# One step of a hybrid decoder on one core: the squares of a sublayer's input go to TensorE one block at a time, without VectorE's sum of two

## The chip, the core and the metric

The kernel runs on one core of one Trainium2 chip. Five engines work from programs of their own and meet only at semaphores: TensorE (PE in the profile, PEld for its weight loads), VectorE (DVE), ScalarE (ACT), GpSimd (POOL) and SyncE (SP), which issues most of the transfers. The metric is the device time of one execution in microseconds (us).

## What is computed

One inference step of a trunk with two layers. Layer 0 is gated linear attention and a convolutional FFN, layer 1 is multi-head latent attention and a convolutional FFN. There are 544 tokens: a prompt of 512 and 8 sequences of 4 new tokens each. The model width is 1024. Around every sublayer stand two norms, one on its input and one on its output:

```python
def rmsnorm(x, g):
    xf = x.astype(jnp.float32)
    y = xf * lax.rsqrt(jnp.mean(xf * xf, axis=-1, keepdims=True) + EPS)
    return (y * g.astype(jnp.float32)).astype(x.dtype)
...
        x = x + rmsnorm(mix, p['norm_mix_post'][l])
        h = rmsnorm(x, p['norm_ffn_pre'][l])
        f, buf = conv_ffn(h, conv_s0[l], p['ffn_w_gate'][l], p['ffn_w_up'][l], p['ffn_conv_w'][l],
                          p['ffn_conv_b'][l], p['ffn_w_down'][l])
        conv_bufs.append(buf)
        x = x + rmsnorm(f, p['norm_ffn_post'][l])
```

What matters here is the mean of x*x over the 1024 channels, one number per token, for the norm on a sublayer's input.

## The kernel before

**Layout.** Channels lie on the 128 partitions, in DC = 8 blocks, and tokens along the free dimension, 544 of them in two halves of HALF = 272. So a sum over channels is a sum over partitions and blocks. TensorE makes it by multiplying with a 128x128 matrix of ones (`ones_matmuls`, line 2128: one matmul for each half, which the program runs as two passes, so that a step shows as x4 in the profile) and adding up the blocks in PSUM, in `px`. ScalarE turns it into rstd = (mean + eps)^-0.5 by a logarithm and an exponential (`rstd`, lines 817 to 822).

**Precision.** Weights and inputs of the large products are split into a high and a low part. A tile of 128 output channels takes, for each of the 8 blocks of input, three products (high by high, high by low, low by high) in two halves: six matmuls (`tile_matmuls`, line 2063) into the bank set `lin`. The input parts are `xg_h` (ACT, line 802, x times the gain) and `xg_l` (DVE, line 1341). rstd is not in them; it is multiplied in where the products leave PSUM, so products can start before rstd is known, but can't leave without it. The weight panels are split too: ACT makes `w_h` (line 791), POOL makes `w_l` (line 669), in two slots each.

**The stage of the change** is the passage from one sublayer to the next. It is gone through with this code in three places: before the first ConvFFN (norm number n = 2, near 302 us), before the latent attention (n = 4, near 703 us) and before the second ConvFFN (n = 8, near 1119 us). Each engine has its own order, written by hand in its part of the program:
- DVE (`next_input`): for block after block, the next-but-one block's normed output `tb` (line 1517), `xg_l` of this block, and x + tb (line 1523). After every second block it adds the squares of the two blocks (line 1572).
- ACT (`next_input`): for each block `xg_h`, then its square into `sq` (line 808). `sq` has two buffers, used in turn. ACT waits on the semaphore `sq_used` until the buffer of the square two before is free.
- PE (`first_panels`): the tile matmuls of the first weight panel as the blocks' `xg_l` arrive; after every second block the ones matmuls on the sum of two squares (`pair_squares`). The tile matmuls of the second panel run LAG = 4 blocks behind. Only the first two blocks' first halves were made ahead, at the end of the stage before.

The norms that are summed in this way are in BY_PAIR; the others go another way, by a running sum in `ssq` and the function `stat`. SQ_BASE and SQ_LEN count the squares through the whole program, and `sq_used` goes up by one for each square: for a pair, once by DVE's sum and once by the ones matmuls.

```python
                    act.wait_ge(sq_used, i - 1)
                fn(sq[:, i % 2, :], src, ACT.Square).then_inc(sq_done, 1)
```

Behind the stage, in a ConvFFN, eight plain panels run on PE, while DVE, ACT and POOL make operands for the paired products that follow (line 2349). The third panel waits until DVE has taken the first tile out of PSUM, with rstd (lines 1595 to 1597). Before the latent attention, ACT makes rstd and then copies the third weight panel.

Of the kernel before, what the change touches and what calls it, by code (L numbers as in the profile page):

```python
# [20 lines left out]
ALU = mybir.AluOpType  # L21
# [5 lines left out]
DC = D // P  # L27
# [66 lines left out]
SQ_BASE = [0, 8, 16, 24, 32, 40, 42, 45, 53, 61]  # L94
SQ_LEN = [8, 8, 8, 8, 8, 2, 3, 8, 8, 8]
# [28 lines left out]
def trunk_program(nc, io):  # L124
    ctx = ExitStack()
    with ctx:
        def sem(name):
            return ctx.enter_context(nc.semaphore(name))
# [12 lines left out]
        def keep(name, shape, dt=F32):  # L141
            off = pos[0]
            pos[0] += (4 * int(np.prod(shape[1:])) + 31) // 32 * 32
            return at(name, off, shape, dt)
# [16 lines left out]
        sq = keep("sq", [P, 2, NT])  # L161
# [126 lines left out]
        def col(name, k=0, n=1):  # L288
            return par[:, PCOL[name] + k:PCOL[name] + k + n]
# [11 lines left out]
        sq_done, sq_used = sem("sq_done"), sem("sq_used")  # L301
# [163 lines left out]

        BY_PAIR = (2, 4, 8)
        DVE_LAST = (0, 3, DC - 1)
        LAG = 4  # L470

        def sums_before(n):

            return sum(k not in BY_PAIR for k in range(n))

        sc_bank = (banks[1], banks[7], banks[0], banks[2])

# [9 lines left out]
        def rest(ch, ahead=AHEAD):  # L487

            return second if ch < ahead else slice(0, NT)
# [816 lines left out]
        def _(dve):  # L1306
            v = nc.vector
# [212 lines left out]
            def add_residual(event, ch):  # L1520
                dve.wait_ge(t_done, DC * event + ch + 1)
                tok = rest(ch)
                v.tensor_tensor(x[:, ch, tok], x[:, ch, tok], tb[:, ch % 2, tok], ALU.add).then_inc(x_done, 1)  # L1523
# [32 lines left out]
            def next_input(event, n, t_last, y, y_gain, split_event, gain, i0):  # L1556
                dve.wait_ge(rstd_done, n + 1)
                residual(event, n, t_last, y, y_gain, 0)
                residual(event, n, t_last, y, y_gain, 1)
                add_residual(event, 0)  # L1560
                add_residual(event, 1)
                for ch in range(DC):
                    if ch < DC - 2:
                        residual(event, n, t_last, y, y_gain, ch + 2)
                    split_x_lo(xg_h, xg_l, ch, col(gain[0], gain[1] + ch), DC * split_event + ch + 1,
                               rest(ch))
                    if ch < DC - 2:
                        add_residual(event, ch + 2)
                    if ch % 2:
                        i = i0 + ch  # L1570
                        dve.wait_ge(sq_done, i + 1)
                        v.tensor_tensor(sq[:, i % 2, :], sq[:, (i - 1) % 2, :], sq[:, i % 2, :], ALU.add).then_inc(sq_used, 1)

            def ffn(layer, pa, ta, pb, tb_, n_stat):
                f0, us0, ps_, ts_ = layer * FC, layer * US_ALL, pa + 2 * PLAIN, ta + 2 * PLAIN
# [471 lines left out]
        def _(pe):  # L2047
# [47 lines left out]
            def first_panels(p, t, arrive, n, halves_from=None):  # L2095

                take_panel(p)
                free_set(t)  # L2100
                if halves_from is not None:
                    for k in range(AHEAD):
                        pe.wait_ge(h_lo, AHEAD * (halved(halves_from) - 1) + k + 1)
                        tile_matmuls(p % 2, t % 2, xg_h, xg_l, (k,), w0=k, start=k == 0, stop=False, halves_=(0,))
                for k in range(DC + LAG):
                    if k < DC:
                        part = dict(w0=k, start=k == 0, stop=k == DC - 1)
                        if halves_from is not None and k < AHEAD:
                            part["halves_"] = (1,)
                        pe.wait_ge(xl_done, arrive + k + 1)  # L2110
                        last = tile_matmuls(p % 2, t % 2, xg_h, xg_l, (k,), **part)
                        if k == DC - 1:
                            last.then_inc(w_used, 1)
                        if n in BY_PAIR and k % 2:
                            pair_squares(n, k)
                    if k == DC and n not in BY_PAIR:
                        stat(n)
                    if k == LAG:
                        take_panel(p + 1)
                        free_set(t + 1)  # L2120
                    if k >= LAG:
                        j = k - LAG
                        last = tile_matmuls((p + 1) % 2, (t + 1) % 2, xg_h, xg_l, (j,), w0=j, start=j == 0, stop=j == DC - 1)
                last.then_inc(w_used, 1)

            def ones_matmuls(src, start, stop):
                for half in range(2):
                    last = mm(px[:, half, 0:HALF], ones[:], src[:, half * HALF:(half + 1) * HALF], start=start, stop=stop)  # L2128
                return last

            def pair_squares(n, k):

                if k == 1:
                    pe.wait_ge(stat_ln, n)
                pe.wait_ge(sq_used, SQ_BASE[n] + k)
                ones_matmuls(sq[:, (SQ_BASE[n] + k) % 2, :], k == 1, k == SQ_LEN[n] - 1).then_inc(sq_used, 1)

            def stat(n):

# [705 lines left out]
```

## Time and profile before

| | us |
|---|---|
| median of 3 runs | 1530.73 |
| lowest and highest | 1529.43, 1531.11 |
| the profiled execution | 1527.54 |
| its span | 1525.8 |
| PE busy (share of the span) | 1446.5 (95%) |
| PE weight loads busy | 1320.1 (87%) |
| DVE busy | 921.5 (60%) |
| ACT busy | 675.2 (44%) |
| POOL busy | 564.2 (37%) |

The span is the time between the first and the last recorded work; the execution's own time is 1.7 us more. Each number in a profile comes from this one execution. A busy share is a mean over stages with different limits, so what counts for an edit is which wait ends last in its own stage. Matmul ends are modelled, and overlap: the distance from one start to the next tells what one costs in a row, and the duration of one also holds its drain. PEclk is the granted clock of TensorE as a share of 2.4 GHz. "[1.62 <-DVE sq L1572]" behind a row means that the engine was idle for 1.62 us before it, until DVE's instruction of line 1572 on `sq` released it.

### The profile page before, as it was taken

To read this page: it belongs to the slowest core of one execution; us is meant where nothing else is said; L and a number is where in the kernel's file an instruction comes from. 1 tells how busy PE (TensorE), PEld (TensorE's weight loads), DVE (VectorE), ACT (ScalarE), POOL (GpSimd) and SP (SyncE) were. 2 spreads that over 40 slices of the span, in tenths; PEclk is the share of its full clock that TensorE was granted. 3 is DMA by queue.
4 is the path that set the end of the run, shared out by engine and by line. 5 is a ranking of instruction groups with operands and counts; after the bars stand their busy time and mean duration, and the time that the engine had idled before them with its cause. 6 is when DMAs were issued, how large, how long until landed. Compare 5 with 4: busy or idle time off the path is not lost.

```text
span 1525.8 us, 31329 instructions
## 1 busy us (share of the span) xinstructions
PE 1446.5 (95%) x11260; PEld 1320.1 (87%) x11260; DVE 921.5 (60%) x1496; ACT 675.2 (44%) x1263; POOL 564.2 (37%) x561
## 2 busy tenths in 40 slices
PE   6999999899999999998899999998979999999997
PEld 6999998799999999997886556665969999999996
DVE  4632436589888882225657744443579888885223
ACT  5333435355666662215412544443254566665211
POOL 2432113335445444341330044441425454544333
PEclk9999999999999999999999999999999999999999
DMA  4242222213232322223221089980212323222221
GB/s 160 71 138 97 111 70 97 88 56 108 87 110 82 110 76 77 95 84 113 75 91 45 1 264 285 284 260 29 84 47 97 111 82 110 82 76 94 95 89 70
DMA packets 55610, 160.20 MB, mean 105 GB/s; under 512 B 7553, under 2 KB 25474, under 8 KB 54226
## 3 DMA queue, kind: packets, MB, share of 16 engines
q1 hardware_dynamic: 49362, 137.82, 27.3%
q0 software_dynamic: 6144, 20.98, 4.6%
q8 instruction: 67, 1.10, 0.3%
q14 instruction: 37, 0.30, 0.1%
HBM read 150.72 MB, written 8.05 MB: 104 GB/s over the span
## 4 chain that ended last, share of the span: by engine, by line
PE 78%; DVE 12%; ACT 4%; issue 3%; POOL 1%; DMA 0%; SPq 0%; ACTq 0%; DVEq 0%; POOLq 0%
PE lin L2063 36%; PE lin L2349 22%; PE lin L2545 4%; PE px L2622 2%; PE px L2586 2%; PE px L2533 1%; PE px L2590 1%; DVE x L1523 1%; DVE tb L1517 1%; PE px L2262 1%; PE px L2553 1%; PE px L2128 1%; DVE xg_l L1341 1%; PE lin L2499 1%; DVE c L1586 1%
## 5 line engine op out<-in xcount | busy, mean ns | idle before, releaser
L674 POOL TENSOR_TENSOR w_l<-w_raw,w_h 128x1024 fp32r<-128x1024 f32 (+1 forms) x62 | 174.6, 2815 | 355.7 <-ACT w_h L791 234.2
L2063 PE MATMUL lin<-xg_h,w_h 128*128 128x272 f32 x960 | 224.1, 309 | 34.1 <-DVE xg_l L1341 26.0
L2063 PE MATMUL lin<-xg_l,w_h 128*128 128x272 f32 x960 | 208.5, 292 | 0.0
L2063 PE MATMUL lin<-xg_h,w_l 128*128 128x272 f32 x960 | 208.1, 292 | 0.0
L2063 PEld LDWEIGHTS lin<-xg_h,w_h 128*128 128x128 f32 x960 | 158.1, 193 | 46.9 <-DVE xg_l L1341 20.2
L2349 PE MATMUL lin<-xq_h,wq_r 128*128 128x272 f32 x864 | 179.9, 296 | 5.5 <-ACT part L1040 5.4
L669 POOL TENSOR_TENSOR w_l<-w_raw,w_h 128x1024 fp32r<-128x1024 f32 (+2 forms) x39 | 98.0, 2513 | 214.0 <-ACT w_h L791 214.0
L791 ACT ACTIVATE w_h<-w_raw 128x1024 fp32r<-128x1024 f32 (+2 forms) x77 | 83.6, 1087 | 210.2 <-PE lin L2063 191.6
L2349 PE MATMUL lin<-xq_h,w_h 128*128 128x272 f32 x576 | 166.2, 289 | 0.3
L2349 PE MATMUL lin<-xq_h,w_l 128*128 128x272 f32 x576 | 166.0, 288 | 0.0
L2349 PE MATMUL lin<-xq_l,w_h 128*128 128x272 f32 x576 | 165.4, 287 | 0.0
L2063 PEld LDWEIGHTS lin<-xg_l,w_h 128*128 128x128 f32 x960 | 157.7, 193 | 0.3
L2063 PEld LDWEIGHTS lin<-xg_h,w_l 128*128 128x128 f32 x960 | 156.4, 192 | 0.0
L2063 PE MATMUL lin<-a_h,w_h 128*128 128x272 f32 x704 | 152.1, 293 | 4.5 <-DVE a_l L1714 4.5
L2349 PEld LDWEIGHTS lin<-xq_h,wq_r 128*128 128x128 f32 x864 | 142.1, 191 | 12.8 <-issue 11.3
L2063 PE MATMUL lin<-a_l,w_h 128*128 128x272 f32 x704 | 150.1, 289 | 0.0
L2063 PE MATMUL lin<-a_h,w_l 128*128 128x272 f32 x704 | 149.7, 289 | 0.0
L2349 PE MATMUL lin<-xq_l,wq_r 128*128 128x272 f32 x432 | 125.7, 291 | 0.0
L456 POOL DMA_DIRECT2D pages<-cache x128 | 68.8, 538 | 150.1 <-issue 142.4
L2063 PEld LDWEIGHTS lin<-a_h,w_h 128*128 128x128 f32 x704 | 112.5, 190 | 5.2 <-DVE a_l L1714 5.0
L2063 PEld LDWEIGHTS lin<-a_l,w_h 128*128 128x128 f32 x704 | 113.5, 190 | 0.2
L2063 PEld LDWEIGHTS lin<-a_h,w_l 128*128 128x128 f32 x704 | 112.5, 189 | 0.0
(360 smaller groups left out, 3111.4 us busy)
## 6 DMA issues: line engine op xcount, KB each, us to landing
wq_raw<-w SPq DMA_DIRECT2D x36, 1024.0 KB, 4.9
w_raw<-w SPq DMA_DIRECT2D x67, 512.0 KB, 3.5
w_raw<-w SPq DMA_DIRECT2D x30, 704.0 KB, 4.1
pages<-cache SPq DMA_DIRECT2D x128, 160.0 KB, 3.8
pages<-cache POOLq DMA_DIRECT2D x128, 160.0 KB, 3.8
St<-state SPq DMA_DIRECT2D x4, 1024.0 KB, 5.2
gla_s<-St SPq DMA_DIRECT2D x4, 1024.0 KB, 3.9
w_raw<-w SPq DMA_DIRECT2D x4, 576.0 KB, 4.1
```

What stands on the lines that cost most here:

```text
L456: eng.dma_start(pages[k][:, j * ROW:(j + 1) * ROW], io["cache"][page, :, cols]).then_inc(ready[k], 16)
L669: g.tensor_tensor(w_l[:, p % 2, 0:n], raw_panel(p)[:, 0:n], w_h[:, p % 2, 0:n].bitcast(F32), ALU.subtract).then_inc(w_lo, 1)
L674: g.tensor_tensor(w_l[:, p % 2, 0:n], w_raw[:, p % 2, 0:n], w_h[:, p % 2, 0:n].bitcast(F32), ALU.subtract).then_inc(w_lo, 1)
L791: fn(w_h[:, p % 2, 0:n], raw_panel(p)[:, 0:n], ACT.Copy).then_inc(w_hi, 1)
L1341: v.scalar_tensor_tensor(out=l_[:, ch, tok], in0=x[:, ch, tok], scalar=gain, in1=h_[:, ch, tok].bitcast(F32), op0=ALU.mult, op1=ALU.subtra ...
L1517: v.scalar_tensor_tensor(out=by_rstd(tb[:, ch % 2, :], tok)[0], in0=y_, scalar=col(gain[0], gain[1] + ch), in1=r_, op0=ALU.mult, op1=ALU.m ...
L1523: v.tensor_tensor(x[:, ch, tok], x[:, ch, tok], tb[:, ch % 2, tok], ALU.add).then_inc(x_done, 1)
L2063: last = mm(lin[:, 2 * out_set + half, 0:HALF], w[:, slot, (w0 + k) * P:(w0 + k + 1) * P], (v[ch] if isinstance(v, list) else v[:, ch, :]) ...
L2349: last = mm(lin[:, out, 0:HALF], w[n][:, k * P:(k + 1) * P], v[n][:, k, :], start=start and k == 0 and m == 0, stop=stop and k == 3 and m ...
L2545: last = nc.tensor.transpose(k_bank(g, r)[:, j * P:(j + 1) * P], latent(g, j, r * P, (r + 1) * P), ident[:])
L2586: mm(s_bank[32 * j:32 * j + 32, :], qabs[:, r, b, :], k_t[:, j, r, :], start=r == 0, stop=False, tile_position=(0, 32 * j))
L2622: last = mm(o_part[32 * j:32 * j + 32, :], p_t[:, kk, 32 * j:32 * j + 32], latent(4 * u + kk, j), start=kk == 0, stop=kk == 3 and u % 2 == ...
```

## The change

The squares of norms 2, 4 and 8 are summed block by block. DVE's sum of two squares is left out, and PE multiplies every block's squares with ones: eight steps in a stage for four. The step for block k - 1 stands behind the tile matmuls of block k, and the last one behind those of the last block. It waits on `sq_done` (the square is written) and not on `sq_used` (the sum is made). `sq_used` still goes up by one for each square, now by PE alone, so ACT's waits read the same but are answered by another engine. The table BY_PAIR gets another name with the same values.

```diff
-        BY_PAIR = (2, 4, 8)
+        ONE_BY_ONE = (2, 4, 8)
...
-                    if ch % 2:
-                        i = i0 + ch
-                        dve.wait_ge(sq_done, i + 1)
-                        v.tensor_tensor(sq[:, i % 2, :], sq[:, (i - 1) % 2, :], sq[:, i % 2, :], ALU.add).then_inc(sq_used, 1)
...
-                        if n in BY_PAIR and k % 2:
-                            pair_squares(n, k)
-                    if k == DC and n not in BY_PAIR:
+                    if n in ONE_BY_ONE and 1 <= k <= DC:
+                        one_square(n, k - 1)
+                    if k == DC and n not in ONE_BY_ONE:
                         stat(n)
...
-            def pair_squares(n, k):
-
-                if k == 1:
+            def one_square(n, k):
+
+                if k == 0:
                     pe.wait_ge(stat_ln, n)
-                pe.wait_ge(sq_used, SQ_BASE[n] + k)
-                ones_matmuls(sq[:, (SQ_BASE[n] + k) % 2, :], k == 1, k == SQ_LEN[n] - 1).then_inc(sq_used, 1)
+                pe.wait_ge(sq_done, SQ_BASE[n] + k + 1)
+                ones_matmuls(sq[:, (SQ_BASE[n] + k) % 2, :], k == 0, k == SQ_LEN[n] - 1).then_inc(sq_used, 1)
```

PE in the first of the three stages, from the last tile matmuls of block 1 (line 2063 before, 2059 now) to those of block 3; the waits are those of each instruction. Before:

```order
L2063 MATMUL lin<-xg_h,w_l 128x272
L2128 MATMUL px<-sq,ones 128x272 [waits sq_used,stat_ln]
L2128 MATMUL px<-sq,ones 128x272
L2063 MATMUL lin<-xg_h,w_h 128x272 [waits xl_done]
L2063 MATMUL lin<-xg_h,w_h 128x272
L2063 MATMUL lin<-xg_l,w_h 128x272 x2
L2063 MATMUL lin<-xg_h,w_l 128x272 x2
L2063 MATMUL lin<-xg_h,w_h 128x272 [waits xl_done]
```

The same place now:

```order
L2059 MATMUL lin<-xg_h,w_l 128x272
L2124 MATMUL px<-sq,ones 128x272 [waits sq_done,stat_ln]
L2124 MATMUL px<-sq,ones 128x272
L2059 MATMUL lin<-xg_h,w_h 128x272 [waits xl_done]
L2059 MATMUL lin<-xg_h,w_h 128x272
L2059 MATMUL lin<-xg_l,w_h 128x272 x2
L2059 MATMUL lin<-xg_h,w_l 128x272 x2
L2124 MATMUL px<-sq,ones 128x272 [waits sq_done]
L2124 MATMUL px<-sq,ones 128x272
L2059 MATMUL lin<-xg_h,w_h 128x272 [waits xl_done]
```

A ones step stands behind block 1 in both, now on the square of block 0 alone; a second one now stands between blocks 2 and 3, where the tile matmuls of the two blocks followed each other.

DVE in the same stage, from xg_l of block 1 to xg_l of block 2. Before:

```order
L1341 SCALAR_TENSOR_TENSOR xg_l<-x,par,xg_h 128x272 [waits xh_done]
L1523 TENSOR_TENSOR x<-x,tb 128x544 [waits t_done]
L1572 TENSOR_TENSOR sq<-sq 128x544 [waits sq_done]
L1517 SCALAR_TENSOR_TENSOR tb<-y_mix,par,px 128x544 [waits x_done]
L1341 SCALAR_TENSOR_TENSOR xg_l<-x,par,xg_h 128x544 [waits xh_done]
```

Now:

```order
L1341 SCALAR_TENSOR_TENSOR xg_l<-x,par,xg_h 128x272 [waits xh_done]
L1523 TENSOR_TENSOR x<-x,tb 128x544 [waits t_done]
L1517 SCALAR_TENSOR_TENSOR tb<-y_mix,par,px 128x544 [waits x_done]
L1341 SCALAR_TENSOR_TENSOR xg_l<-x,par,xg_h 128x544 [waits xh_done]
```

The sum is gone and nothing else moved. The order of ACT, POOL and SP is unchanged.

## Rows read from the trace of the kernel before

**Rows 1.** Page, part 4: share of each engine in the chain that ended last.
```profile
PE 78%; DVE 12%; ACT 4%; issue 3%; POOL 1%; DMA 0%; SPq 0%; ACTq 0%; DVEq 0%; POOLq 0%
```

**Rows 2.** Lines 2128 and 1572: count, ns min/median/max, first and last start, form.
```profile
L2128 PE MATMUL px<-sq,ones x60: 390/392/793, 25.6 to 1136.7; 128*128 128x272 f32 x60
...
L1572 DVE TENSOR_TENSOR sq<-sq x12: 714/718/724, 305.1 to 1134.0; 128x544 f32<-128x544 f32 x12
```

**Rows 3.** Chain in 299 to 345: start us, us, work.
```profile
305.14 0.64 DVE sq L1572
```

**Rows 4.** Timeline, first stage: start, us, engine, work [idle before, releaser].
```profile
304.56 0.60 PE L2063 MATMUL lin<-xg_h,w_h 128*128 128x272 f32 x1 [0.70 <-DVE xg_l L1341]
...
305.06 0.72 DVE L1572 TENSOR_TENSOR sq<-sq 128x544 f32<-128x544 f32 x1
...
305.69 0.77 DVE L1517 SCALAR_TENSOR_TENSOR tb<-y_mix,par,px 128x544 f32<-128x544 f32 x1
305.81 0.66 ACT L808 ACTIVATE sq<-x 128x544 f32<-128x544 f32 x1 [1.62 <-DVE sq L1572]
...
305.92 2.15 PE L2128 MATMUL px<-sq,ones 128*128 128x272 f32 x4 [0.31 <-DVE sq L1572]
306.37 0.73 ACT L802 ACTIVATE xg_h<-x,par 128x544 fp32r<-128x544 f32 x1
306.38 0.78 DVE L1341 SCALAR_TENSOR_TENSOR xg_l<-x,par,xg_h 128x544 fp32r<-128x544 f32 x1
307.08 0.71 DVE L1523 TENSOR_TENSOR x<-x,tb 128x544 f32<-128x544 f32 x1
...
307.72 0.77 DVE L1517 SCALAR_TENSOR_TENSOR tb<-y_mix,par,px 128x544 f32<-128x544 f32 x1
...
308.11 0.66 ACT L808 ACTIVATE sq<-x 128x544 f32<-128x544 f32 x1 [1.01 <-PE px L2128]
308.32 0.66 PE L2063 MATMUL lin<-xg_l,w_h 128*128 128x272 f32 x2
...
308.77 0.66 PE L2063 MATMUL lin<-xg_h,w_l 128*128 128x272 f32 x2
...
311.89 0.52 PE L2063 MATMUL lin<-xg_h,w_h 128*128 128x272 f32 x2
...
312.25 0.42 PE L2063 MATMUL lin<-xg_l,w_h 128*128 128x272 f32 x2
...
312.51 0.41 PE L2063 MATMUL lin<-xg_h,w_l 128*128 128x272 f32 x2
...
319.24 1.08 PE L2128 MATMUL px<-sq,ones 128*128 128x272 f32 x4
...
320.46 0.70 ACT L817 ACTIVATE rstd_x<-px,par 128x544 f32<-128x544 f32 x1
```

**Rows 5.** Stretches: length, busy us (instructions) of each engine, PEclk, DMA share, GB/s.
```profile
309.00:310.00 1.00, 1.00 (x5) 0.88 (x5) 1.00 (x3) 0.41 (x1) 0.00 (x0) 0.50 0.00 0
310.00:311.00 1.00, 1.00 (x7) 0.96 (x6) 1.00 (x2) 0.51 (x1) 0.00 (x0) 0.72 0.00 0
...
709.00:710.00 1.00, 1.00 (x6) 0.87 (x5) 1.00 (x3) 0.94 (x2) 0.00 (x0) 0.54 1.01 426
```

**Rows 6.** Timeline behind the stage: DVE in the first, PE in the second.
```profile
322.54 0.44 DVE L1595 TENSOR_TENSOR u<-lin,rstd_x 128x272 f32<-128x272 f32 x1 [4.61 <-ACT rstd_x L822]
...
323.21 0.18 DVE L1597 TENSOR_TENSOR u<-lin,rstd_x 128x32 f32<-128x32 f32 x1
...
725.75 0.52 PE L2063 MATMUL lin<-xg_h,w_h 128*128 128x272 f32 x2 [1.11 <-POOL w_l L669]
```

**Rows 7.** Stretches behind: two of the first ConvFFN, one of attention.
```profile
360.00:370.00 10.00, 9.70 (x75) 9.26 (x75) 9.98 (x12) 6.94 (x12) 4.64 (x4) 1.00 0.24 69
370.00:380.00 10.00, 7.79 (x55) 7.27 (x54) 8.43 (x14) 5.15 (x10) 4.57 (x8) 0.94 0.23 67
...
900.00:920.00 20.00, 20.00 (x233) 13.17 (x229) 8.48 (x18) 8.97 (x22) 9.21 (x18) 1.00 0.93 286
```

More of the change, by code:

```diff
@@ L472, in sums_before @@
         def sums_before(n):
-            return sum(k not in BY_PAIR for k in range(n))
+            return sum(k not in ONE_BY_ONE for k in range(n))
         sc_bank = (banks[1], banks[7], banks[0], banks[2])
```

## Prediction

> **What bounds the kernel now.** I read the page first: TensorE (PE) holds 78% of the chain that ended last, VectorE (DVE) 12% [rows 1]. So the edit, which takes work from DVE and gives work to PE, has to be judged only where PE waits for DVE. Line 1572 runs 12 times [rows 2], in three stages of four: at about 302 us (input of the first ConvFFN), 703 us (input of the latent attention) and 1119 us (input of the second ConvFFN). They read alike, so I work out the first and correct for the other two.
>
> The chain of work in that stage shows DVE without a gap to 315.15, and three sums of two squares are links of it, 0.64 us each or within 0.01 of that; the first is shown [rows 3]. Then the chain crosses to the ones matmuls (line 2128) and leaves the stage through ScalarE (ACT): weight copy, logarithm, rstd. The timeline [rows 4] gives the prices and shows three engines locked together:
> - DVE, per block of 128 channels: tb, xg_l, x. The next instruction starts 0.69, 0.70 and 0.64 us after the one before (305.69, 306.38, 307.08, then 307.72), 2.03 us for a block; a sum adds 0.63 (305.06 to 305.69).
> - ACT, per block: xg_h, then the square, in program order. A square lasts 0.66 us and xg_h of the next block starts 0.56 us after it (305.81 to 306.37). So a square that waits holds back the next block's xg_h, hence its xg_l, hence its tile matmuls.
> - PE. At the low clock a pair of tile matmuls takes 0.45 us (308.32 to 308.77), so the six of a block 1.37 us; the four passes of one ones step take 2.15 us with the last one's drain, which is 0.79 of it [rows 2, 4]: 0.453 each, 1.81 us for the step. At the full clock it is 0.25 for a pair (312.25 to 312.51), 0.75 for a block, and 1.08 with a drain of 0.39, so 0.91 for a ones step. The granted clock is 0.50 through 310 and half way up in the slice after it, so it rises near 310.6; in the second stage it rises near 709.9 [rows 5], 6.6 us after that stage's first matmuls against 7.7 here. 0.50 is the 1.2 GHz level, 1.00 the 2.4 GHz one.
>
> **What the edit removes.** Twelve sums. Of each four, three lie on DVE's unbroken stream: 3 x 0.63 = 1.9 us earlier for the xg_l of block 6. The fourth follows DVE's last xg_l and nothing needs DVE after it, so it is worth nothing. If that were all, three stages would give 3 x 1.9 = 5.7 us.
>
> **What it adds.** Ones steps: eight for four in each stage, 4 x 0.91 = 3.6 us of PE at the full clock. And it changes who frees the two buffers of sq. Before, the buffer for square 2 is freed by the first sum on DVE, which ends before PE has even begun the ones step (305.78 against 305.92). Now PE frees it, and ones step 0 stands behind the tile matmuls of block 1. The loop is: ones step k ends, square k+2 (0.56), xg_h of k+3 (0.74), xg_l (0.78), with about 0.04 us at each crossing 2.2 us, then tile matmuls k+3, which stand in front of ones step k+2.
>
> Walked through with those prices, in this trace's times:
> - Block 1's matmuls start at 304.56 as before and leave PE free at 305.24. Ones step 0 starts there (DVE's 0.7 us of waiting is gone) and takes 1.81, done with its drain at 307.4.
> - Square 2 starts at 307.44, where it was 305.81. xg_h of block 3: 308.00, was 306.37. DVE meanwhile has no sum to do and runs dry for the first time.
> - PE: block 2 from 307.06 to 308.42, ones step 1 to 310.23, drained at 310.57. Square 3 starts at 310.61, was 308.11. xg_h of block 4 at 311.17; its xg_l from 311.95 to 312.73.
> - Block 4's matmuls start at 312.8, were 311.89: 0.9 later, although DVE had 1.3 us less to do.
> - From there PE has no gap: blocks 4 to 7 of the first panel (4 x 0.75), ones steps 3 to 7 (5 x 0.91), blocks 0 to 3 of the second panel (4 x 0.75) come to 10.55 us. The last ones step is through at 323.35. Before, it went from 319.24 to 320.15 [rows 4]: 8.26 us after 311.89, of which 7.1 were work and 1.2 waits for DVE.
>
> So the last ones step is through 3.2 to 3.3 us later in this stage. With the clock rising 6.6 us after the first matmuls, as in the second stage, the same walk gives 2.9. The same walk made for the kernel before lands within 0.15 us of its own trace for the last ones step, and it gives the same end for any rise between 306 and 311: before, DVE sets the pace and the clock is hidden; after, PE sets it and the clock shows.
>
> **What is behind it.** rstd waits for the last ones step and everything behind it waits for rstd. In the second stage directly: the logarithm starts as the ones step ends, the next weight panel is copied behind it on ACT, GpSimd splits it and PE, already idle, takes it at 725.75 [rows 6]. All of the delay passes. In the ConvFFN stages the logarithm is 0.14 us late today (320.46 against 320.32), behind a weight copy [rows 4], which is then done earlier than needed: 0.1 us absorbed. Then DVE starts at 322.54, after 4.61 us of waiting for rstd [rows 6], on a stretch that it nearly fills (9.98 us of 10 from 360 to 370, 8.43 of the next 10) and that carries on to 382, where the chain goes back to PE; PE is busy for only 7.79 us from 370 to 380 [rows 7]. DVE's ramp starts later by the whole delay, so PE does too. DVE's product with rstd, which the third panel waits for, is out at 323.39 [rows 6], and PE comes free near 323.9 (320.15 and five blocks of 0.75), so there is half a microsecond of slack; and PE is itself 2.1 to 2.5 us late there; nothing can be won back from it. In the attention stage a delay could vanish behind transfers, as their share is 0.93, but PE is busy 20.00 of 20 there [rows 7]: it sets the pace and passes the delay on.
>
> **Sum.** 3.2 + 2.9 + 2.8 = 8.9 us with the rises of this trace. But each stage now starts at another moment, and in another run the clock may rise elsewhere. Bounds: at the full clock from the start the walk gives 1.15 us per stage (PE's added steps alone, past the 1.2 us of waits that they fill and what the earlier DVE gives), with the latest rise 3.3. I take 2.85 per stage less 0.1 twice, 8.4 us, near the upper bound, because both rises lie at 6.6 to 7.7 us. Against the profiled execution (1527.54, span 1525.8) that is 1535.9. The median of the three runs is 3.2 us above that execution, so the forecast is 1530.73 + 8.4 = 1539.1, or 0.55% slower.
>
> **Rivals.**
> - The clock rises sooner. For it: ones step 0 fills a wait, so PE is busy from 304.56 on without a gap. Against it: in the trace the clock stayed at 0.50 until past 310 [rows 5], though PE had worked nearly throughout since 305.92. A rise 2 to 4 us sooner in the walk gives 1.5 to 2.2 us per stage, 4.5 to 6.5 us in all: 1535.2 to 1537.2. The Trainium skill, TensorE: Matmul & The Clock Gate, Part 1, says that the slow clock is the default and that activity releases it. By that rule the denser stream can only help, and the sum would be that of this rival instead of 8.4; the trace agrees that the rise comes in the midst of dense work, and shows no case as dense as the new one.
> - No measurable change: full clock nearly from the start, 1.15 per stage, 3.4 us, or a part of the delay hidden behind PE's panels in the ConvFFN ramps, which PE entered only 0.5 us behind rstd's product. 1532 to 1534. For it, only that the ramps are loose enough to hold 2.2 us of PE waits; against it, that these are waits for DVE, whose stream is the delayed one.
> - Faster: DVE stays the pace of the stage. It holds if ones step k is over when ACT is ready for square k+2. Then each stage ends 1.9 us sooner, 5.7 in all, 1525.0. The point that decides is 305.7: square 2 must start there or before. Ones step 0 can't start before block 1's xg_l at 304.50 and takes 0.91 us even at the full clock, so it would have to run ahead of block 1's matmuls, which the program's order forbids. The sums are links of the chain [rows 3], which is all that speaks for it.
> - The edit reaches less than it says: only the three stages above hold line 1572, and the order of DVE and PE shows all twelve gone and twelve ones steps more; I give this nothing.
>
> **How the numbers follow.** A difference of 0.2% (3.1 us) is about what a measurement of this kernel can tell from none. Forecast, 6.5 to 10 us later: 0.66. Clock sooner, 3.5 to 6.5 later: 0.18. No measurable change: 0.09. Faster: 0.05. Slower than all of this, if each crossing between engines costs PE more than I took (24 waits of ones steps) or the clock falls back in a stage: 0.02. Faster by over 0.2% 0.05, within it 0.10, slower 0.85. The range leaves out the last, the faster one and most of no change: 1534.7 to 1541.5.
>
> **What would show it.** Right: squares 2 and 3 wait for the ones matmuls and start 1.5 to 2.5 us later after the stage's first matmuls than now; DVE has gaps in the stage; PE has none from block 4 on; the last ones step is through about 20.5 us after 302.82 where it was 17.3; DVE's wait for rstd grows from 4.61 us by more than 3 (its stream ends sooner too); PE waits about 4 us instead of 1.1 for the panel near 725. Wrong: the granted clock at 1.00 within 4 us of the stage's start; squares that wait for nothing; or a full delay at rstd of which less is left where the paired products of the ConvFFN start, 60 us on.

## The result, and the profile after

The changed kernel took 1536.95 us (median of five runs, 1535.58 to 1540.85) against 1529.62 (1528.62 to 1531.11) for the kernel before: ratio 1.0054, 95% interval 1.0043 to 1.0065. It is slower by half a per cent; the forecast was 1539.1, the range 1534.7 to 1541.5. The profiled execution took 1535.58 (span 1533.9), which is 8.1 us more of span than before. The medians of the runs below leave out a few executions that took far longer, 1792.90 us in the mildest case.

Page of the changed kernel, parts 1 and 4 (before: [rows 1] and the table of times):

```profile
PE 1454.0 (95%) x11308; PEld 1327.3 (87%) x11308; DVE 913.7 (60%) x1484; ACT 675.6 (44%) x1263; POOL 564.9 (37%) x561
...
PE 80%; DVE 10%; ACT 4%; issue 3%; POOL 1%; DMA 0%; SPq 0%; ACTq 0%; DVEq 0%; POOLq 0%
```

DVE's busy time fell by 7.8 us and PE's rose by 7.5, and the span followed PE. The source view of line 2124 (2128 before) shows the steps that were added and who waits for them now:

```profile
L2124 PE MATMUL px<-sq,ones x108: 390/392/661, 24.1 to 1144.9; 128*128 128x272 f32 x108
...
who waited for it (us, times):
  ACT sq L808: 25.0, 18
```

The same entry in the kernel before, where the squares waited for two lines, first that of line 1572 (DVE's sum), then that of line 2128 (the ones matmuls):

```profile
  ACT sq L808: 13.9, 9
```

```profile
  ACT sq L808: 3.0, 3
```

There were 60 of these passes before [rows 2], so 48 more, twelve ones steps of four. ACT's squares waited 25.0 us for them, in 18 places, six in each of the three stages. They had waited 16.9 us in 12 places before, so most of this waiting isn't new.

I compare the stages by times from a stage's first tile matmul: 302.82 in the kernel before, 301.32 in the changed one. Timeline of the changed kernel, first stage (columns as in [rows 4]):

```profile
301.32 0.59 PE L2059 MATMUL lin<-xg_h,w_h 128*128 128x272 f32 x1 [3.66 <-DVE xg_l L1341]
...
303.90 2.02 PE L2124 MATMUL px<-sq,ones 128*128 128x272 f32 x4
...
305.96 0.66 ACT L808 ACTIVATE sq<-x 128x544 f32<-128x544 f32 x1 [3.27 <-PE px L2124]
...
307.29 0.78 DVE L1341 SCALAR_TENSOR_TENSOR xg_l<-x,par,xg_h 128x544 fp32r<-128x544 f32 x1 [0.93 <-ACT xg_h L802]
...
308.85 0.66 ACT L808 ACTIVATE sq<-x 128x544 f32<-128x544 f32 x1 [1.60 <-PE px L2124]
...
311.02 0.52 PE L2059 MATMUL lin<-xg_h,w_h 128*128 128x272 f32 x2 [0.54 <-DVE xg_l L1341]
...
316.76 0.79 DVE L1341 SCALAR_TENSOR_TENSOR xg_l<-x,par,xg_h 128x544 fp32r<-128x544 f32 x1 [1.65 <-ACT xg_h L802]
...
319.18 1.08 PE L2124 MATMUL px<-sq,ones 128*128 128x272 f32 x4
...
319.89 0.61 PE L2059 MATMUL lin<-xg_h,w_h 128*128 128x272 f32 x2
...
320.85 1.08 PE L2124 MATMUL px<-sq,ones 128*128 128x272 f32 x4
...
324.06 0.44 DVE L1591 TENSOR_TENSOR u<-lin,rstd_x 128x272 f32<-128x272 f32 x1 [6.51 <-ACT rstd_x L822]
```

Square 2 starts at +4.64 us (305.96 less 301.32), where it was at +2.99 and waited for DVE's sum [rows 4]; it waits for the ones matmuls now. Square 3 is at +7.53 instead of +5.29, block 4's matmuls at +9.70 instead of +9.07, the last ones step starts at +19.53 instead of +16.42 and its record, drain included, ends at +20.61 instead of +17.50. DVE, which had no gap before up to the xg_l of block 6, waits for xg_h. Between the last two ones steps now stands a block of the second panel's tile matmuls (319.89); before, that block (the second panel's block 3) stood behind the last ones step. DVE's first product with rstd is at +22.74 instead of +19.72.

The chain of the changed kernel through the stage (start, us, what) now lies on PE, where it lay on DVE up to 315.15 before. Once it leaves PE, for the way from a ones step over a square, xg_h and xg_l to block 4's matmuls:

```profile
307.28 1.55 PE px L2124 x4
308.85 0.66 ACT sq L808
309.51 0.64 ACT xg_h L802
310.18 0.80 DVE xg_l L1341
311.02 1.02 PE lin L2059 x6
...
321.01 0.93 PE px L2124 x4
321.96 0.72 ACT rstd_x L817
...
384.26 5.77 PE lin L2345 x44
```

Its last row shows that nothing is won back on the way: the first paired product of the chain starts 82.94 us after the stage's first matmul. In the chain of the kernel before it is this piece, 79.90 us after it:

```profile
382.72 17.30 PE lin L2349 x134
```

So 3.04 us of delay arrive, of 3.02 that entered. The other two stages read alike. In the table "rise" is when the granted clock comes back to 1.00, worked out from slices of 1 us.

| stage | rise, before / after | end of last ones record, before / after | DVE's product with rstd, delay |
|---|---|---|---|
| 1 | +7.74 / +7.08 | +17.50 / +20.61 | 3.02 |
| 2 | +6.56 / +6.34 | +17.50 / +20.25 | 2.74 |
| 3 | +6.72 / +5.64 | +17.49 / +19.92 | 2.33 |

The delays add up to 8.09 us, which is the difference of the spans. Two other differences lie outside the stages and cancel. In the first stretch the 48 matmuls at 17 us are 1.5 us shorter in the changed kernel's profile; at 738 us a piece of the same kind is 1.5 us longer. Chain of the changed kernel, then of the kernel before:

```profile
17.03 6.33 PE lin L2059 x48
...
738.30 7.79 PE lin L2059 x48
```

```profile
17.01 7.83 PE lin L2063 x48
...
734.09 6.27 PE lin L2063 x48
```

Both kernels do the same work there. Where the piece is longer the granted clock was down: 0.79 from 17 to 25 us in the kernel before, and in the changed one these stretches (columns as in [rows 5]):

```profile
738.00:739.00 1.00, 0.70 (x4) 0.73 (x5) 1.00 (x3) 0.00 (x0) 1.00 (x1) 0.74 0.82 328
739.00:740.00 1.00, 1.00 (x6) 1.00 (x6) 1.00 (x1) 0.00 (x0) 1.00 (x1) 0.50 0.05 21
```

A comparison of one profile with one profile can therefore be out by 1.5 us from a stretch that has nothing to do with the edit, which is why I read the experiments stage by stage as well as by their ratio.

### The profile page after: what moved, and what is told of

It is laid out like the page before. It is cut to its first block, busy times and chain, and to the rows that moved or that the text cites. A ratio compares the mean times of both kernels' runs of the same rounds, so it can differ in the third digit from the quotient of the medians.

```text
span 1533.9 us, 31413 instructions
## 1 busy us (share of the span) xinstructions
PE 1454.0 (95%) x11308; PEld 1327.3 (87%) x11308; DVE 913.7 (60%) x1484; ACT 675.6 (44%) x1263; POOL 564.9 (37%) x561
## 4 chain that ended last, share of the span: by engine, by line
PE 80%; DVE 10%; ACT 4%; issue 3%; POOL 1%; DMA 0%; SPq 0%; ACTq 0%; DVEq 0%; POOLq 0%
PE lin L2059 37%; PE lin L2345 22%; PE lin L2541 4%; PE px L2618 2%; PE px L2124 2%; PE px L2582 2%; PE px L2529 1%; PE px L2586 1%; PE px L2258 1%; PE px L2549 1%; PE lin L2495 1%; DVE c L1582 1%; DVE xn L1626 1%; DVE xs_l L1341 1%; ACT w_h L791 0%
```

## The experiments

The theory has three parts: PE has more to do in a stage; the low clock of the stage's first microseconds, which was hidden behind DVE, now counts; and a loop through the two buffers of `sq` (ones step, square, xg_h, xg_l, tile matmuls, next ones step) can hold PE back. Rivals: the added PE work alone explains it, with neither loop nor clock; or the moved squares delay things elsewhere. Each run is compared with the kernel before on the same chip. "Last ones" is the end of the last ones record after the stage's first tile matmul, in the three stages.

| run | ratio, 95% interval | last ones | rise of the clock |
|---|---|---|---|
| changed kernel, above | 1.0054 [1.0043, 1.0065] | 20.61, 20.25, 19.92 | 7.08, 6.34, 5.64 |
| e0_after | 1.0067 [1.0054, 1.0080] | 20.89, 20.43, 19.93 | 7.96, 6.72, 5.68 |
| e1_early | 1.0019 [1.0010, 1.0028] | 17.78, 18.48, 17.78 | 3.34, 5.48, 2.90 |
| e2_dead_sums | 1.0060 [1.0047, 1.0073] | 20.51, 20.37, 20.54 | 6.74, 6.10, 6.78 |
| e3_half_ones | 0.9987 [0.9978, 0.9996] | 17.26, 17.26, 17.23 | 7.70, 6.68, 7.22 |
| e5_fp32r | 0.9981 [0.9972, 0.9989] | 16.57, 16.50, 16.10 | 10.12, 9.94, 9.04 |
| e6_warm_after | 1.0022 [1.0013, 1.0031] | 18.82, 18.83, 18.81 | up throughout |
| e7_warm_before | 0.9999 [0.9990, 1.0008] | 17.50, 17.50, 17.50 | up but for 3.48 to 6.88 in stage 1 |
| e9_warm_early | 1.0004 [0.9995, 1.0013] | 17.77, 17.77, 17.77 | up throughout |
| e4_one_pair | 0.9993 [0.9984, 1.0002] | 17.31, 16.86, 16.85 | 8.50, 5.98, 6.00 |
| e10_more_ones | 1.0023 [1.0013, 1.0034] | 18.31, 18.30, 18.31 | 3.72, 4.16, 3.90 |
| e8_warm_fp32r | 0.9967 [0.9955, 0.9980] | 15.38, 16.07, 15.86 | falls inside, back at 7.18, 9.98, 9.50 |

**The changed kernel again.** No edit.

> The changed kernel again, beside the others on the same chip. The walk gives 2.2 to 3.3 us a stage, 7 to 9.5 us over the kernel before, and an end of each stage that follows the moment at which the granted clock rises: the last ones step is through about 0.5 us later for each microsecond that the clock rises later. If the delay were a fixed price of twelve ones steps (12 x 0.91 = 10.9 us less the waits they fill), it would be the same in each stage whatever the clock does.

1538.41 us against 1528.87. The delay repeats. Its stages and the first run's make six points, and they order by the rise alone: 5.64 and 5.68 give 19.92 and 19.93, 6.34 gives 20.25, 6.72 gives 20.43, 7.08 gives 20.61, 7.96 gives 20.89. That is 0.3 to 0.5 us of delay for each microsecond by which the clock rises later. The kernel before has rises from 6.56 to 7.74 and 17.49 to 17.50 in all of them.

**The order: ones step ahead of the next block's matmuls.** The ones step of block k-1 is moved in front of block k's tile matmuls.

```diff
+                        if n in ONE_BY_ONE and k:
+                            one_square(n, k - 1)
                         pe.wait_ge(xl_done, arrive + k + 1)
                         last = tile_matmuls(p % 2, t % 2, xg_h, xg_l, (k,), **part)
...
-                    if n in ONE_BY_ONE and 1 <= k <= DC:
+                    if n in ONE_BY_ONE and k == DC:
```

> The changed kernel with each ones step put ahead of the tile matmuls of the next block instead of behind them. Nothing is added or taken away. If the delay comes in part from the loop through the two buffers of sq (ones step k, square k+2, xg_h, xg_l, tile matmuls k+3), the shorter loop gives back 0.9 to 1.3 us a stage: 3.0 to 3.9 us faster than the changed kernel, still 3 to 6 us slower than the kernel before, and square 2 starts at 3.0 us after the stage's first matmuls where it is 4.64 now. If the delay is only PE's added work, the time is that of the changed kernel within 1 us.

It ran 1531.48 us, 6.9 less than the changed kernel on the same chip; 3.0 to 3.9 was expected. Square 2 starts 2.90 us after the first matmul (304.26 less 301.36), as expected, and the first squares wait half as long as in the changed kernel or less (the last two still wait 1.37 and 1.12 us):

```profile
301.36 0.59 PE L2059 MATMUL lin<-xg_h,w_h 128*128 128x272 f32 x1 [3.65 <-DVE xg_l L1341]
...
304.26 0.66 ACT L808 ACTIVATE sq<-x 128x544 f32<-128x544 f32 x1 [1.54 <-PE px L2126]
...
305.82 0.66 ACT L808 ACTIVATE sq<-x 128x544 f32<-128x544 f32 x1 [0.26 <-PE px L2126]
...
318.06 1.08 PE L2126 MATMUL px<-sq,ones 128*128 128x272 f32 x4
```

The size is off because the clock moved too. A stretch of the same run:

```profile
304.00:305.00 1.00, 1.00 (x6) 0.95 (x5) 1.00 (x3) 0.74 (x2) 0.00 (x0) 0.65 0.00 0
```

PE is busy without a gap from the first matmul on, and the clock is up after 3.34 us instead of 7 to 8. The run shows that most of the loss goes with the order of two steps on PE, but it mixes order and clock. The next three take them apart.

**The clock held up.** In PE's wait ahead of each stage, 26 matmuls are put whose result nothing reads. One edit, in the changed kernel (e6), in the kernel before (e7) and in the early order of e1 (e9):

```diff
+                if n in (2, 4, 8):
+                    pe.wait_ge(stat_ln, n)
+                    for _ in range(26):
+                        mm(px[:, 0, 0:HALF], w_h[:, p % 2, 0:P], w_h[:, p % 2, 0:HALF], start=True, stop=True)
                 for k in range(DC + LAG):
```

> The changed kernel with 26 idle matmuls (272 columns, result overwritten) in each of the three stages, in the 3.7 us in which PE waits ahead of the first tile matmuls, so that the granted clock should not fall. If the low clock makes most of the delay, the last ones step is through 18.7 us after the stage's first matmuls (20.4 now, 17.5 in the kernel before) and the time is 3 to 4 us over the kernel before. If the clock is of no account, it stays 7 to 9 us over it.

> The kernel before with the same 26 idle matmuls in each stage. The walk says that DVE sets the pace there and the clock is hidden: the last ones step stays at 17.4 to 17.5 us and the time within 1 us of the kernel before. If the low clock costs in that kernel too, it gets 2 us or more faster.

> The changed kernel with both remedies: ones steps ahead of the next block's tile matmuls and the idle matmuls that keep the granted clock up. What is left of the delay is PE's added work. The walk gives a last ones step at 17.7 to 17.9 us into each stage, against 17.5 in the kernel before and 18.8 with the idle matmuls alone: 0.5 to 1.3 us slower than the kernel before. If the two remedies gave back the same microseconds, it stays at 18.8 and 3.3 us slower.

First matmul and last ones record of the first stage, with the starts of block 1 and block 4 in two of them, in e6, then e7, then e9:

```profile
302.48 0.39 PE L2059 MATMUL lin<-xg_h,w_h 128*128 128x272 f32 x1 [0.33 <-DVE xg_l L1341]
...
304.22 0.39 PE L2059 MATMUL lin<-xg_h,w_h 128*128 128x272 f32 x1 [1.09 <-DVE xg_l L1341]
...
310.39 0.52 PE L2059 MATMUL lin<-xg_h,w_h 128*128 128x272 f32 x2 [0.18 <-DVE xg_l L1341]
...
320.22 1.08 PE L2128 MATMUL px<-sq,ones 128*128 128x272 f32 x4
```

```profile
302.81 0.39 PE L2063 MATMUL lin<-xg_h,w_h 128*128 128x272 f32 x1 [0.33 <-DVE xg_l L1341]
...
319.24 1.08 PE L2132 MATMUL px<-sq,ones 128*128 128x272 f32 x4
```

```profile
302.66 0.39 PE L2059 MATMUL lin<-xg_h,w_h 128*128 128x272 f32 x1 [0.33 <-DVE xg_l L1341]
...
303.14 1.08 PE L2130 MATMUL px<-sq,ones 128*128 128x272 f32 x4
304.40 0.39 PE L2059 MATMUL lin<-xg_h,w_h 128*128 128x272 f32 x1 [0.18 <-DVE xg_l L1341]
...
310.47 0.52 PE L2059 MATMUL lin<-xg_h,w_h 128*128 128x272 f32 x2
...
319.36 1.08 PE L2130 MATMUL px<-sq,ones 128*128 128x272 f32 x4
```

And the clock in e6:

```profile
302.00:306.00 4.00, 2.36 (x12) 1.48 (x10) 4.00 (x8) 1.96 (x5) 0.00 (x0) 1.00 0.34 120
306.00:310.00 4.00, 3.67 (x20) 2.86 (x20) 3.99 (x7) 2.42 (x4) 0.00 (x0) 1.00 0.00 0
```

With the clock at 1.00 the changed kernel's stages end at 18.82, thrice and within 0.02, where they ended between 19.92 and 20.89. The kernel before stays at 17.50 whether the clock is up or not, and takes the same time (0.9999). So the low clock costs the changed kernel 1.1 to 2.1 us per stage and the kernel before nothing. All three runs came out as expected; e9 as a whole (1.0004) can't be told from the kernel before.

The 1.32 us that are left at the full clock (18.82 less 17.50), and the 1.05 of them that the order of e9 takes (18.82 less 17.77), can be read from two distances: from the first matmul to the start of block 4's, and from there to the start of the last ones step (us, range over the stages).

| run | block 4 starts at | from there to the last ones step |
|---|---|---|
| kernel before | 9.07 to 9.08 | 7.34 to 7.35 |
| e7_warm_before | 9.08 | 7.34 to 7.35 |
| changed kernel, both runs | 9.00 to 9.98 | 9.82 to 9.84 |
| e6_warm_after | 7.90 to 7.91 | 9.83 to 9.84 |
| e9_warm_early | 7.80 to 7.81 | 8.89 |
| e10_more_ones | 9.07 to 9.09 | 8.15 to 8.16 |

- The low clock acts ahead of block 4 alone, as it has risen by then: 9.00 to 9.98 where it is 7.91 with the clock up.
- Behind block 4 the changed kernel is 2.48 us longer at either clock. Seven blocks and one ones step stood there before, eight blocks and four steps do now: three steps of 0.91 and one block of 0.75 more, less about 1.0 us of waits that they fill.
- Ahead of block 4 the changed kernel is 1.16 us shorter at the full clock, since two sums have left DVE's stream. 2.48 less 1.16 is the 1.32.
- Of the 1.05 that e9 takes, 0.94 lies behind block 4 and is one ones step: e6 has PE waiting 1.09 us ahead of block 1, e9 puts the step on block 0 into that wait, and three steps instead of four are left behind block 4. The loop through `sq` can have no more than the other 0.10, by which block 4 starts later in e6.

At the low clock the loop costs more, but not much: PE's wait ahead of block 4 is 0.26 to 0.54 us in the changed kernel's six stages, 0.18 in e6 and about 0.2 in the kernel before. No run takes the loop away by itself, as a third buffer of `sq` would. Nor was the last ones step put back ahead of the second panel's block 3; by the block's price, an estimate, that would be worth up to 0.75 us per stage.

**Do the sums matter at all?** DVE's four additions of a stage are put back into the changed kernel, as dead work into `ssq`; PE's part stays.

```diff
+                    if ch % 2:
+                        if event or ch > 1:
+                            dve.wait_ge(dead, 4 * event + ch // 2)
+                        v.tensor_tensor(flat(ssq[:]), x[:, ch - 1, :], x[:, ch, :], ALU.add).then_inc(dead, 1)
+                dve.wait_ge(dead, 4 * event + 4)
```

> The changed kernel with DVE's four additions a stage put back as dead work: same shape and place, on other data, with nobody waiting for the result. If DVE is off the path now, as the walk has it, they cost 0.1 to 0.6 us a stage, at most 2 us in all, against the 1.9 us a stage that they held on the path in the kernel before. If DVE still sets the pace, 4 to 6 us come back on top of the changed kernel's time.

1539.43 us against 1529.82: 1.0060, inside the span of the changed kernel's own two ratios. Its stages end at 20.51 and 20.54 with rises of 6.74 and 6.78, where the changed kernel has 20.43 at 6.72, and at 20.37 with a rise of 6.10, where the line between the changed kernel's points gives about 20.1. So the 1.9 us per stage that the edit takes off DVE's stream are worth 0.1 to 0.2 us per stage there: DVE waits for ACT anyway.

**PE's work halved, order kept.** Each ones step covers one half of the tokens only (the sums of squares miss the other half), so twelve steps' worth of PE time goes and waits and order stay.

```diff
-                ones_matmuls(sq[:, (SQ_BASE[n] + k) % 2, :], k == 0, k == SQ_LEN[n] - 1).then_inc(sq_used, 1)
+                ones_matmuls(sq[:, (SQ_BASE[n] + k) % 2, :], k < 2, k >= SQ_LEN[n] - 2, (k % 2,)).then_inc(sq_used, 1)
```

> The changed kernel with each ones step cut to one half of the tokens (even blocks the first half, odd blocks the second), so that PE does as much in ones steps as in the kernel before; the sums of squares of these three norms miss the other half. DVE still makes no sums and ACT still waits for PE. If PE's added work is the main price, the stage ends 0.0 to 0.7 us earlier than in the kernel before and the time is 0 to 2 us below it. If the waits of ACT for PE were the price by themselves, most of the 7 to 8 us would stay.

1526.40 us. By the ratio's interval that is 0.6 to 3.4 less than the kernel before on that chip, by the medians 2.5; 0 to 2 was expected. The stages give 0.7 of it (17.25 for 17.50, three times); where the rest lies stayed open, since the profile's stretches outside the stages differ by more than that from run to run. What it tells: with PE's amount of ones work as before, the new order, the new release of `sq` and DVE's gain together cost nothing net.

**The ones step made shorter.** Squares and ones are written in the rounded 4-byte form that the large products use, so that a step is two matmuls and not four passes.

```diff
-        ones = keep("ones", [P, P])
+        ones_r = keep("ones_r", [P, P], F32R)
...
-                    square(i0 + ch, x[:, ch, :])
+                    square(i0 + ch, x[:, ch, :], sq_r)
...
-                ones_matmuls(sq[:, (SQ_BASE[n] + k) % 2, :], k == 0, k == SQ_LEN[n] - 1).then_inc(sq_used, 1)
+                ones_matmuls(sq_r[:, (SQ_BASE[n] + k) % 2, :], k == 0, k == SQ_LEN[n] - 1, ones_r[:]).then_inc(sq_used, 1)
```

> The changed kernel with the squares of these norms written, and multiplied with ones, in the rounded fp32 form that the tile matmuls use, so that a ones step is two matmuls instead of four passes; by the pair of tile matmuls in the trace, 0.25 us at the full clock and 0.45 at the low one, for 0.91 and 1.81. The walk then gives a last ones step 1.5 to 1.8 us earlier than in the kernel before in each stage, and PE's end 2.3 to 2.6 earlier: 4.5 to 5.5 us faster than the kernel before, 12 to 13 faster than the changed one. If ACT's waits for PE keep their length whatever a ones step costs, it stays slower than the kernel before.

1525.81 us, 3.1 less than the kernel before, where 4.5 to 5.5 less was expected. The stages end 0.9 to 1.4 sooner than before. Its timeline, and below it a stretch, show the short step and a granted clock that stayed down to between +9.0 and +10.1, longer than in any run with full-precision ones steps:

```profile
305.08 0.66 PE L2128 MATMUL px<-sq_r,ones_r 128*128 128x272 f32 x2
306.25 0.82 PE L2063 MATMUL lin<-xg_h,w_h 128*128 128x272 f32 x2 [0.52 <-DVE xg_l L1345]
```

```profile
311.00:312.00 1.00, 1.00 (x6) 1.00 (x6) 1.00 (x3) 0.79 (x2) 0.00 (x0) 0.50 0.00 0
```

A ones step is 0.66 us with its drain here where it was 2.02, and PE has waits again, as the second row shows. So one block at a time with a short step beats the kernel before. Whether it is the better way as such isn't shown: the kernel before, with its pairs and the short step, was not run, and may gain as much.

**One pair only.** In the kernel before, blocks 2 and 3 alone are summed one by one, with their steps early; one sum of four goes.

```diff
+        SINGLE = (2, 3)
...
-                    if ch % 2:
+                    if ch % 2 and ch not in SINGLE:
...
+                        if n in BY_PAIR and k - 1 in SINGLE:
+                            one_square(n, k - 1)
                         pe.wait_ge(xl_done, arrive + k + 1)
```

> The kernel before with the edit made for one pair alone, blocks 2 and 3: their squares go to PE one at a time, each step ahead of the next block's tile matmuls, and DVE adds the other three pairs. One sum of 0.63 us leaves DVE's stream and one ones step of 0.91 joins PE's, which has 1.2 us of waits at the full clock. The walk gives a last ones step 0.5 to 0.6 us earlier than in the kernel before in each stage (17.5 there): 1.4 to 1.9 us faster. If any one-by-one step costs more than the sum that it replaces, it is 1 us or more slower.

The last ones record comes 0.64 us sooner in two stages (16.86) and 0.19 in the one where the clock rose at +8.50. That is the length of one sum, as one sum less on DVE's stream should give. As a whole 1527.60 against 1528.83, where 1.4 to 1.9 less was expected; 0.9993 with an interval that holds 1: not told apart from no change.

**PE's added work alone.** In the kernel before, four ones steps of 240 columns each, whose result nothing reads, go behind the even blocks; `sq` and DVE's sums stay as they are.

```diff
+                        if n in BY_PAIR and k % 2 == 0:
+                            if k == 0:
+                                pe.wait_ge(stat_ln, n)
+                            for half in range(2):
+                                mm(px[:, half, HALF:512], ones[:], par[:, 0:240], start=False, stop=False, skip_group_check=True)
```

> The kernel before, DVE's sums and all, with four dead ones steps a stage more on PE (240 columns for 272, behind the tile matmuls of the even blocks, waiting for nothing): PE's added work of the change without its waits. The walk gives a last ones step 0.8 to 0.9 us later (18.3 for 17.5): 2.4 to 2.8 us slower than the kernel before, a third of the changed kernel's delay. If PE's added work were the whole price, it would be 7 to 9 us slower.

The stages end at 18.31, 18.30 and 18.31: 0.81 more than before, as expected, and a quarter to a third of the changed kernel's 2.4 to 3.4. By the table of distances, the two steps ahead of block 4 cost nothing, as they fall into PE's waits, and the two behind it 0.81 together. So the amount of added work alone doesn't explain the delay; where it stands, and the clock (e6), do. One thing the run leaves open: its clock was back after 3.7 to 4.2 us, so it doesn't show what the same steps cost under a low clock of 7 us. The time rose by 4.0 us, where the stages hold 2.4 and 2.4 to 2.8 was expected. The profile shows low clocks elsewhere that this edit does not touch, as here (the kernel before has 1.00 in this stretch):

```profile
720.00:740.00 20.00, 16.84 (x117) 16.27 (x116) 13.28 (x12) 10.55 (x15) 7.85 (x3) 0.91 0.21 71
```

Whether that is all of the rest, one profile can't say.

**The best of all together.** Short ones step, early order and the 26 matmuls.

> The two-matmul ones steps (squares in the rounded form), each ahead of the next block's tile matmuls, and the idle matmuls ahead of the stage. In the run of the two-matmul steps alone the clock rose only 9 to 10 us into the stage and the last ones step was through at 16.1 to 16.6. With the clock kept up the walk gives 15.3 to 15.5, 2.0 us a stage under the kernel before: 5.5 to 6.5 us faster than it, 2.5 to 3.5 faster than the steps alone. If that run had nothing left to gain from the clock, the two are the same.

1525.52 us against 1529.82, 4.3 less: faster than both kernels, but by less than the 5.5 to 6.5 expected. It has the lowest ratio of the study, though its interval overlaps that of e5, over which 2.5 to 3.5 us were expected. The first stage ends at 15.38, as the walk had it, the other two 0.7 and 0.5 us later than that. Granted clock in its first stage:

```profile
303.00:306.00 3.00, 1.59 (x10) 1.14 (x9) 3.00 (x6) 2.50 (x5) 0.00 (x0) 1.00 0.31 128
...
307.00:308.00 1.00, 1.00 (x6) 1.00 (x6) 1.00 (x3) 0.75 (x1) 0.00 (x0) 0.50 0.00 0
```

The matmuls ahead of the stage hold the clock up to its start, but then PE is busy for 1.59 us of 3.00, and the clock falls in the midst of the stage. In e6 and e9, with the long ones steps, the same 26 matmuls were enough.

## Why the prediction was right, step by step

- **Where the edit is judged.** Right: PE's share of the chain went from 78% to 80%, and 1.9 us less on DVE's stream bought 0.1 to 0.2 us per stage (e2). With the clock up it buys more, 1.16 us at block 4 (e6).
- **The walk.** It gave square 2 at +4.62 (measured +4.64), square 3 at +7.79 (+7.53), block 4's matmuls 0.9 us late (0.63), then 10.55 us of PE without a gap to the last ones step (10.74: 321.76 less 311.02). Both differences of the middle terms go with the clock, which rose at +7.08 and not at +7.7. The total, 3.2 to 3.3 us at that rise and 2.9 at 6.6, compares with 3.11 at 7.08 and 3.39 at 7.96.
- **Before, the clock is hidden; after, it shows.** Shown by e6 and e7: 18.82 for about 20.3 with the clock held up, 17.50 for 17.50.
- **The bound at the full clock, 1.15 us per stage.** 1.32 (e6), and by the account given: PE's added steps, past the waits that they fill and what the earlier DVE gives. One part of it was in the walk's count without being called a change: of its eight blocks ahead of the last ones step, only seven stood there before, so 0.75 of the 2.48 us behind block 4 is a block of tile matmuls and not a ones step. The walk's loop through `sq` was there (square 3, then block 4), but it is a small part: at most 0.10 us at the full clock.
- **All of it passes.** 3.02 us enter behind rstd in the first stage and 3.04 arrive at the paired products, 60 us on. The 0.1 us absorbed in the ConvFFN stages is there too: 3.11 at the ones step, 3.02 at DVE.
- **The sum.** 2.85 per stage was taken; the three stages delayed their last ones step by 2.76 on average, and rstd's products by 8.09 us in all, where 8.4 was forecast. The 0.3 between them is the clock, 0.2 to 1.1 us sooner than before in each stage. The median moved by 7.3 us, the repetition by 9.5. Of the 2.15 us between the forecast and the median measured, 1.1 is the kernel before, whose median of five runs is 1529.62 and not 1530.73; that is no merit or fault of the walk.
- **The rival of the clock.** The Trainium skill, TensorE: Matmul & The Clock Gate, Part 1, has activity release the slow clock, which stood behind that rival. The trace agrees in direction: 7.08, 6.34 and 5.64 us where it was 7.74, 6.56 and 6.72. It was not the 2 to 4 us sooner that the rival needed; that took a PE without the wait ahead of block 1 (two stages of e1, and e10).
- **Two signs were wrong.** PE was to wait "about 4 us instead of 1.1" for the panel near 725, and DVE's wait for rstd to grow "by more than 3 (its stream ends sooner too)". PE waited 1.87 us, by the timeline of the second stage (its first matmul is at 704.83):

```profile
729.97 0.52 PE L2059 MATMUL lin<-xg_h,w_h 128*128 128x272 f32 x2 [1.87 <-POOL w_l L669]
```

  The panel came 2.75 us later (25.14 after the first matmul, where 725.75 less 703.36 is 22.39), but PE got there 1.99 us later as well, since the delay is one of its own stream. The text had said so of the ConvFFN stages and left it out of the sign. The 0.76 between the two is the block of 0.75 that now stands ahead of the last ones step: five blocks followed it before, four do now. DVE's wait grew by 1.90 (6.51 for 4.61 [rows 6]): its stream ended 1.12 us later in the stage, not sooner, since its last xg_l waits 1.65 us for an xg_h that stands behind a waiting square. The step that failed is "its stream ends sooner too"; it had the sums leave DVE and forgot that DVE's last blocks wait for squares that wait for PE. The time doesn't hang on it.

## What to carry to other kernels

Count what comes to stand ahead of the last link, and where. At the full clock this edit loses because three ones steps and a block of tile matmuls more stand behind block 4, where PE has little waiting left to fill; one of the steps, put into PE's wait ahead of block 1, cost 0.94 us per stage less (e9), and in e10 the two dead steps ahead of block 4 cost nothing. Before moving work onto the engine that holds 78% of the chain, look also at whether its slow-clock stretches are hidden today: held up, the clock gave this edit 1.1 to 2.1 us per stage back and the kernel before nothing (e6, e7). Don't take a long wait for its cost: the squares waited 25.0 us for PE, and the loop behind it held at most 0.10 us per stage at the full clock. And shorten the step before multiplying it: with a ones step of two matmuls the same edit is 3 us faster than the kernel before, instead of 7 to 9 slower.

## What the runs showed of the hardware

- The moment at which the granted clock comes back ranged far wider than I had assumed, and mostly with what PE did in the stage. Counted from the first matmul: 2.9, 3.3 and 5.5 us in e1, where PE is busy without a gap (3.30 us of the first 3.30, 5.48 of the first 5.48); 3.7 to 4.2 in e10, with dead steps in the waits; 5.6 to 8.5 in the kernels with waits in between (6.41 us busy of the first 7.10 in the changed kernel); 9.0 to 10.1 in e5 (8.70 of 10.10). The stages of one run differ by up to 2.6 us (e1) at the same order of work, so PE's work doesn't fix the moment by itself. An edit that makes PE's work lighter can get part of its gain taken back (e5, e8), and one that makes it denser can get more than it was due (e1).
- In e8 the clock fell within a stage, 3.2 to 6.1 us after its first matmul, with PE at work on and off all the while; in e7 it did in one stage of three, 3.5 us in.
- The same 48 matmuls took 6.3 or 7.8 us from one execution to the next, by the granted clock alone (17 us and 738 us, above). That is half of what this study could tell from no change.
